# The first pieces of input and weight on one queue, in the order in which TensorE takes them

## The reference, cut to what matters

```python
def rmsnorm(x, g):
    xf = x.astype(jnp.float32)
    y = xf * lax.rsqrt(jnp.mean(xf * xf, axis=-1, keepdims=True) + EPS)
    return (y * g.astype(jnp.float32)).astype(x.dtype)

def swiglu_ffn(x, w_gate, w_up, w_down):
    return (jax.nn.silu(x @ w_gate) * (x @ w_up)) @ w_down

def first_block(x, ...):
    x = x + 0.5 * swiglu_ffn(rmsnorm(x, ffn1_norm[l]), ffn1_w_gate[l], ffn1_w_up[l], ffn1_w_down[l])
    x = x + hybrid_mixer(rmsnorm(x, mix_norm[l]), w_in[l], ...)      # chunked attention and pooling
    x = x + 0.5 * swiglu_ffn(rmsnorm(x, ffn2_norm[l]), ffn2_w_gate[l], ffn2_w_up[l], ffn2_w_down[l])
    return rmsnorm(x, final_norm[l])

def second_block(x, ...):                                            # a gated and a sparse attention
    for i in range(DEPTH_2):
        x = _layer_norm(DN_ALPHA * x + mixers[i % N_MIXERS](x), ln_g[i], ln_b[i], LN_EPS)
```

## Time and profile before

| | us |
|---|---|
| median of three runs | 712.92 |
| lowest, highest | 711.59, 713.33 |
| the profiled execution | 714.85 |
| its span (first to last instruction) | 713.0 |
| TensorE busy | 701.6 |
| VectorE busy | 480.7 |
| ScalarE busy | 378.8 |
| GpSimd busy | 58.4 |

### The profile page before, as it was taken

The page is one execution under the profiler, slowest core; times in us unless marked ns, Lnnn a source line. Parts: engine busy times, 40 slices in busy tenths (PEclk is TensorE's granted clock), DMA queues, the critical chain, the costliest instruction groups (busy, mean ns, idle before and its releaser), DMA issues.

```text
span 713.0 us, 9730 instructions
## 1 busy us (share of the span) xinstructions
PE 701.6 (98%) x3728; PEld 596.4 (84%) x3728; DVE 480.7 (67%) x724; ACT 378.8 (53%) x517; POOL 58.4 (8%) x35
## 2 busy tenths in 40 slices
PE   7999999999999999999999999999999999999995
PEld 6888888888888788888888888888888888878884
DVE  5597767755567456877776855466764638898756
ACT  6764445544375655755444644477444534675450
POOL 1000000000000500000000000000005272131001
PEclk8999999999999999999999999999999999999999
DMA  8878455545446305655554556536574183543001
GB/s 308 349 288 319 176 184 197 204 182 182 172 147 262 122 16 194 235 183 199 207 176 176 187 214 250 177 122 232 182 246 159 33 321 119 178 157 139 1 1 59
DMA packets 21635, 129.33 MB, mean 181 GB/s; under 512 B 2584, under 2 KB 4512, under 8 KB 7392
## 3 DMA queue, kind: packets, MB, share of 16 engines
q1 hardware_dynamic: 19872, 126.72, 49.0%
q10 hardware_dynamic: 1488, 1.34, 0.6%
q0 software_dynamic: 240, 0.79, 0.4%
HBM read 127.79 MB, written 1.06 MB: 181 GB/s over the span
## 4 chain that ended last, share of the span: by engine, by line
PE 98%; DMA 1%; DVE 1%; ACT 0%; ACTq 0%; issue 0%
PE ps L419 24%; PE ps L384 16%; PE ps L386 16%; PE ps L385 16%; PE ps L425 13%; PE ps L404 1%; PE ps L564 1%; PE ps L633 1%; DMA raw<-in_gu 1%; PE ps L804 1%; PE ps L982 1%; PE ps L438 1%; PE ps L408 1%; PE ps L580 1%; PE ps L688 1%; PE ps L690 1%
## 5 line engine op out<-in xcount | busy, mean ns | idle before, releaser
L1495 DVE TENSOR_TENSOR wlo<-raw,whi 128x2048 fp32r<-128x2048 f32 x69 | 159.0, 2313 | 39.7 <-ACT whi L1056 39.5
L419 PE MATMUL ps<-xt,whi 128*128 128x512 f32 x752 | 180.1, 391 | 0.0
L1056 ACT ACTIVATE whi<-raw 128x2048 fp32r<-128x2048 f32 x78 | 148.6, 1908 | 44.0 <-PE ps L386 42.1
L419 PEld LDWEIGHTS ps<-xt,whi 128*128 128x128 f32 x752 | 138.2, 188 | 26.6
L384 PE MATMUL ps<-whi,xt 128*128 128x512 f32 (+1 forms) x304 | 121.8, 401 | 0.1
L386 PE MATMUL ps<-whi,xt 128*128 128x512 f32 (+1 forms) x304 | 117.0, 385 | 0.0
L385 PE MATMUL ps<-wlo,xt 128*128 128x512 f32 (+1 forms) x304 | 116.7, 384 | 0.0
L425 PEld LDWEIGHTS ps<-xt,wlo 128*128 128x128 f32 x752 | 96.4, 191 | 3.7
L425 PE MATMUL ps<-xt,wlo 128*128 128x256 f32 x752 | 97.5, 283 | 0.0
L1448 POOL TENSOR_TENSOR wlo<-raw,whi 128x2048 fp32r<-128x2048 f32 (+1 forms) x9 | 41.0, 4557 | 550.5 <-ACT whi L1056 550.5
L1100 ACT ACTIVATE work<-ps 128x512 f32<-128x512 f32 x44 | 26.3, 598 | 96.6 <-PE ps L419 95.5
(11 more groups left out here) (236 smaller groups left out, 703.3 us busy)
## 6 DMA issues: line engine op xcount, KB each, us to landing
raw<-in_gu SPq DMA_DIRECT2D x41, 1024.0 KB, 4.8
raw<-in_dn SPq DMA_DIRECT2D x22, 1024.0 KB, 4.7
raw<-in_win SPq DMA_DIRECT2D x8, 1024.0 KB, 4.8
raw<-in_fqk SPq DMA_DIRECT2D x8, 1024.0 KB, 4.8
raw<-in_wout SPq DMA_DIRECT2D x4, 1024.0 KB, 5.0
raw<-in_fg SPq DMA_DIRECT2D x4, 1024.0 KB, 4.8
raw<-in_fv SPq DMA_DIRECT2D x4, 1024.0 KB, 4.8
raw<-in_fo SPq DMA_DIRECT2D x4, 1024.0 KB, 4.8
```

Of the source, the lines that this page charges most:

```text
L419: return pe.matmul(ps[:, banks[u], :], wh[:, k * S + u * P:k * S + (u + 1) * P], x, start=k == 0, stop=k == KD - 1)
L1056: act.activation(whi[:, c % RING, 0:n], raw[:, c % RING, 0:n], ACT.Copy).then_inc(hi_ready, 1)
L1495: dve.tensor_tensor(wlo[:, c % RING, 0:n], raw[:, c % RING, 0:n], whi[:, c % RING, 0:n].bitcast(F32), ALU.subtract).then_inc(lo_ready, 1)
```

## The change

All transfers of the opening but input pieces 3 and 4 are issued by SP: first `sm`, then for each piece i the input piece (for i below 3), the weight piece of chunk 0 and the weight piece of chunk 1. ACT issues nothing at the start. POOL issues input pieces 3 and 4 alone, both after input piece 0 has landed. `STEPS` alternates between the chunks from the start, and with it the order in which ACT, DVE and PE work. There are eleven idle products instead of nine.

```diff
-STEPS = [(0, 0), (0, 1), (1, 0), (1, 1)] + [(c, i) for i in range(2, len(PIECES)) for c in range(2)]
+STEPS = [(c, i) for i in range(len(PIECES)) for c in range(2)]
...
-            for step, (c, i) in enumerate(STEPS):
+            def x_piece(i):
+                k, n = PIECES[i]
+                sp.dma_start(x_turned[:, k:k + n, :], a["xt"][:, k:k + n, :]).then_inc(xt_landed[i], 16)
+
+            def weight_piece(step):
+                c, i = STEPS[step]
                 k, n = PIECES[i]
                 cols = slice(k * S, (k + n) * S)
-                if step < 2:
-                    sp.dma_start(x_turned[:, k:k + n, :], a["xt"][:, k:k + n, :]).then_inc(xt_landed[i], 16)
-                else:
-                    sp.dma_start(raw[:, c, cols], a["gu0"][c][:, cols]).then_inc(part_landed[step] if step < N_PARTS else raw_landed[c], 16)
+                sp.dma_start(raw[:, c, cols], a["gu0"][c][:, cols]).then_inc(part_landed[step] if step < N_PARTS else raw_landed[c], 16)
+
+            sp.dma_start(sm[:, :], a["sm"]).then_inc(sm_landed, 16)
+            for step, (c, i) in enumerate(STEPS):
+                if c == 0 and i < 3:
+                    x_piece(i)
+                weight_piece(step)
...
-            for _ in range(9):
+            for _ in range(11):
                 pe.matmul(ps[:, DOWN + 3, 0:P], idle, idle, start=True, stop=True)
...
-            act.dma_start(sm[:, :], a["sm"]).then_inc(sm_landed, 16)
-            for step in range(2):
-                act.dma_start(raw[:, 0, step * S:(step + 1) * S], a["gu0"][0][:, step * S:(step + 1) * S]).then_inc(part_landed[step], 16)
...
-            for i in range(2, len(PIECES)):
+            pool.wait_ge(xt_landed[0], 16)
+            for i in range(3, len(PIECES)):
                 k, n = PIECES[i]
-                if i == 3:
-                    pool.wait_ge(xt_landed[0], 16)
                 pool.dma_start(x_turned[:, k:k + n, :], a["xt"][:, k:k + n, :]).then_inc(xt_landed[i], 16)
```

## The result

| | median us (runs) | ratio to before, 95% interval | PE enters the loop in the profile | the profiled execution |
|---|---|---|---|---|
| before | 712.84 (22) | | 33.57; in a second look 31.41 | 714.85; 712.76 |
| after | 714.76 (22) | 1.0026 [1.0019, 1.0033] | 33.91 | 715.21 |

I had forecast 709.0. The change costs 1.9 us instead. The hole of 2.42 us behind the first step is gone, and a longer one stands behind the fourth.

What follows compares the result with a forecast made beforehand. PE, 98% busy, was taken as the bound, its opening hole costing 5.1 us. The first pair ends 4.4 earlier, minus 0.4 row wait and 0.1 idle products: 712.92 - 3.9 = 709.0 us, range 707.6 to 712.3.

Steps and rivals of the forecast that it cites:

- Issues and the first step: Opening: SP issues 0.44 to 0.48 us apart at first; first product at 5.5 to 5.9, a loss up to 0.4.
- Input piece 2: Opening, fifth step: bytes queued on SP over the old rates gave input 2 landing at 7.9, (0,2) at 8.6.
- priced them at 0 to 0.6: POOL's two transfers: input 3, needed at 11.1, lands between 9 and 11.7, costing 0 to 0.6 us; taken as 0.
- the forecast's 7.9 and 24.44: Landing times claimed for input piece 2 (7.9) and for chunk 4 (24.44).
- A gap of 1.1 us at most: PE's wait before the fifth step, which starts about 9.5; claimed far shorter than the old 2.42 us.
- the clock: PE's opening: clock stays full, 0.70 us per unit (one k-step of one chunk); the old half-clock stretch cost 2.7 us.
- rival (a): Opening: a short gap or slower landing drops the clock again; gain only 1.7 to 3.0, 710.6 us; chance 0.20.
- The size of the gain: Whole opening: hole costs 5.1 us, first pair of chunks ends 4.4 earlier, 3.9 us kept after the cap.
- The cap by the row: Chunk 4 lands at 24.44, ACT's row is ready at 26.75; PE enters chunk 4 no earlier than 29.55, losing 0.4.
- Rival (c): Opening: single queue falls behind, first weight lands at 8.0; costs 0.3 to 1.6, 713.2 to 714.5 us; chance 0.08.

Runs made afterwards that it cites:

- experiment 3: The changed kernel with nine idle products instead of eleven: 714.73 us, 1.0025 of before.
- experiment 1: The changed kernel with input pieces 3 and 4 also issued by SP, none by GpSimd (also written e1): 713.67 us, 1.0014 of before.
- e6: The changed kernel with nothing issued by GpSimd, ACT issuing input pieces 1 and 2 and SP the rest: 712.51 us, 1.0005 of before.
- e8: The changed kernel with everything issued by SP, input pieces and chunks 0 and 1's weight pieces contiguous in device memory: 711.71 us, 0.9992 of before.
- e14: The kernel before with contiguous input and small weight pieces; issuers, order and idle products unchanged: 710.86 us, 0.9981 of before.
- e11: The changed kernel, all by SP, contiguous pieces, three idle products before the fifth step, row copied before chunk 4's rounding: 712.08 us, 0.9991 of before.
- e4b: The kernel before with alternating step order alone, its three queues kept: 713.15 us, 1.0010 of before.

## Why the prediction was wrong

**Issues and the first step: right.** SP issued 0.44 to 0.48 us apart, the first product started at 5.78 (forecast 5.5 to 5.9). (0,1) landed at 6.1 and (1,1) at 6.5, forecast 6.1 and 6.8; PE did four units in a row by 9.2 instead of 8.4, since the idle products ran to 6.13 (forecast 5.4 to 5.9); experiment 3 shows that this did not matter.

**Input piece 2: the step that failed.** "Input 2 at 7.9, (0,2) at 8.6": they landed at 10.87 and 11.7. The step divided the bytes ahead in the queue by the rates that before had shown in the same microseconds, 210 GB/s from 5 to 7 and 403 from 7 to 8. A rate that was read at another mix of queues and pieces is not a property of the microsecond: after had 236 and 166. GpSimd's two transfers, which start just then, are measured (about 1 us of the time, experiment 1); I had priced them at 0 to 0.6 by when they themselves are needed, and not by what they take from SP's. The rest goes with the single queue: a second one brings 198 GB/s from 2 to 9 us to 262 and 0.6 us by the ratios (e1 to e6), with intervals that overlap. That three queues were a gain in before I had not seen at all. Together they make up the loss to within what the runs can tell (e6 is at 1.0005 of before).

Rows 8 KB apart are something else. Contiguous pieces bring input piece 2 from 8.9 to 7.5 or 8.4, and are worth 1.6 us from e1 to e8; but they are worth 1.4 us to the kernel before as well (e14). So they tell why the landing of 7.9 was out of reach with one queue, and not why after is slower than before, which has the same rows. That e8 comes near the forecast's 7.9 and 24.44 is no proof of the sum, which took its rates from rows 8 KB apart.

**"A gap of 1.1 us at most", and the clock: fell with it.** The gap was 3.27, and the clock was down for 3.4 us behind it. The rival (a) had the fall right and the gap wrong.

**The size of the gain: mis-sized by the profile.** I took the hole as 5.1 us of every execution. The second look shows 1.06 + 1.75 = 2.8. Even with input piece 2 at 7.9 the gain against such an execution would have been 2.8 us at most, and with the prediction's own cap 31.41 - 29.55 = 1.9, not 3.9. So of the 5.8 us between forecast and result about 2 are this; the fact that the profiled execution stood 1.93 above the median, and above all three runs, was a warning, which I used only as an offset.

**The cap by the row: right as a mechanism, not reached in after.** Its time was too early: chunk 4 landed at 26.7 and not at 24.44, since SP issued it at 17.31 and not at 15.64. The wait shows in e1 (1.01 us), and in e8 (0.44) where chunk 4 lands at 24.7.

**Rival (c), slower, was right in its sign, with another point.** It decided "from a first weight landing at about 7.5"; the first weight landed at 4.2. The queue fell behind later, at its eighth transfer. That its 713.2 to 714.5 lies just under 714.76 is chance.

## What to carry to other kernels

When transfers are put in another order or on another queue, do not take the rates of the old mix as given: put beside the sum the time from issue to landing that the old profile shows behind a backlog (here 6.4 to 6.6 us; input piece 2 then took 6.8), and price each transfer of another queue by the bytes it takes from the piece that is needed next. Where the profiled execution lies outside the timed runs, look at a second one before pricing its largest wait, and see from the granted clock of each execution whether they fall in groups. Lay out small first pieces contiguously: by the ratios this was worth 1.6 us here with one queue and 1.4 with three, about as much as giving the issues back to two queues (1.5 from after to e6).

## What the runs showed of the hardware

- In after and e1 a piece of 128 KB landed 2.3 to 3.1 us after its issue while little was queued, while 256 KB issued at 4.03 took 6.8 us beside GpSimd's transfers, 4.8 without them, and 3.4 (e8) or 4.3 (e11) with contiguous rows as well.
- Rows of 1 to 2 KB, 8 KB apart: the DMA engines were 89% busy at 169 GB/s (e1, 7 to 9 us); contiguous 103% at 368. The Trainium skill, page "DMA: Bandwidth & Descriptors", section "Latency and other measured facts", reports slow copies at row pitches that are large powers of two, 164 GB/s at 2 MiB and 103 at 4 MiB, with contiguous tiles as one of two cures. The cure agrees with e8; the pitch here is far smaller. With one queue the lower rate lasts beyond 10 us (e1 344 GB/s from 12 to 14 us, e8 419), while before reaches 399 GB/s from 8 to 14.8 with the same rows from three queues. Why, no run here settles. I had not expected it.
- The clock fell at or behind holes of 1.06 (the second look at before, where PE had also idled for 1.00 us just before its first product), 1.18 (e4b), 1.83 (e14), 2.42 and 3.27 us, and not behind one of 2.02 (e1). The length of the hole alone does not decide. The lower clock lasted 3.4 us in the second look and in after, and 6.8 in the profile of the earlier trace rows.
- From one execution to the next of the same kernel the landing of the same small pieces differs by about 1 us: the two profiles of before show 8.28 and 7.33 for chunk 0's second piece, and 714.85 and 712.76 us.
